# One encoder layer on one core: output weights split during the column pairs, and a new order of copies, sums and operands in the projection

## The reference, cut to what matters

```python
h = rms_norm(x, p['g_mix'][l])
proj = h @ p['w_in'][l]
hq, hf_fwd, hf_bwd, hi, hg, dq, dk, dv = jnp.split(proj, points, axis=-1)
q_hg = silu(hq);  f = lb + (1 - lb) * sigmoid(fx);  gates = log(f), 1 - f     # fx: hf_fwd, hf_bwd
...
x = x + mix @ p['w_out'][l]
```

## Time and profile before

| What | Value |
|---|---|
| Median of 3 runs | 2064.74 us (2061.48 to 2066.44) |
| The profiled execution | 2061.51 us; its span 2059.7 us |
| TensorE busy | 1958.7 us, 95% |
| VectorE, ScalarE, POOL busy | 72%, 60%, 15% |
| Token steps; column pairs | 0 to 210 us; 210 to 470 us |

### The profile page before, as it was taken

How to read it: one execution, slowest core, us unless ns; L and a number is a source line. 1 busy time by engine, 2 the same in 40 slices (tenths; PEclk the granted TensorE clock), 3 DMA queues, 4 the chain that set the end, 5 groups by cost and what they waited for, 6 DMA issues and landing times. The chain is left out here.

```text
span 2059.7 us, 31859 instructions
## 1 busy us (share of the span) xinstructions
PE 1958.7 (95%) x11162; PEld 1620.1 (79%) x11162; DVE 1491.5 (72%) x2050; ACT 1237.7 (60%) x1974; POOL 307.7 (15%) x394
## 2 busy tenths in 40 slices
PE   7988999999999899999999999999999999999983
PEld 6876887887888667778887888887888888888871
DVE  5347665648999588877311455578999999999976
ACT  5442466526788498744322433327888888888863
POOL 0220012110000021111000000001223332222210
PEclk9999999999999999999999999999999999999997
DMA  6492333446655451334334322448999999999988
GB/s 211 165 308 93 103 123 133 144 161 181 185 177 174 155 191 38 103 134 149 104 123 161 122 101 91 154 150 315 384 384 379 382 376 379 381 385 393 378 310 325
DMA packets 178389, 448.27 MB, mean 218 GB/s; under 512 B 21152, under 2 KB 100384, under 8 KB 151648
## 3 DMA queue, kind: packets, MB, share of 16 engines
q1 hardware_dynamic: 146032, 347.48, 47.3%
q0 software_dynamic: 32240, 99.25, 13.2%
HBM read 366.46 MB, written 94.90 MB: 224 GB/s over the span
## 5 line engine op out<-in xcount | busy, mean ns | idle before, releaser
L113 PE MATMUL cross_ot_ps<-w_w_high,cross_o_high 128*128 128x512 f32 x544 | 219.9, 404 | 2.1 <-DVE w_w_low L2932 1.6
L115 PE MATMUL cross_ot_ps<-w_w_high,cross_o_low 128*128 128x512 f32 x544 | 213.3, 392 | 0.0
L2932 DVE TENSOR_TENSOR cross_low_up<-cross_raw_up,w_w_high 128x2048 fp32r<-128x2048 f32 x68 | 152.8, 2289 | 12.4 <-ACT w_w_high L2716 12.2
L2932 DVE TENSOR_TENSOR cross_low_down<-cross_raw_down,w_w_low 128x2048 fp32r<-128x2048 f32 x68 | 152.7, 2287 | 1.7 <-ACT w_w_low L2716 1.7
L2932 DVE TENSOR_TENSOR w_w_low<-cross_raw_gate,w_w_high 128x2048 fp32r<-128x2048 f32 x68 | 152.3, 2279 | 0.0
L2716 ACT ACTIVATE w_w_high<-cross_raw_up 128x2048 fp32r<-128x2048 f32 x68 | 126.2, 1906 | 0.3 <-issue 0.3
L2716 ACT ACTIVATE w_w_low<-cross_raw_down 128x2048 fp32r<-128x2048 f32 x68 | 126.2, 1906 | 0.0
L2716 ACT ACTIVATE w_w_high<-cross_raw_gate 128x2048 fp32r<-128x2048 f32 x68 | 126.0, 1901 | 0.0
L113 PEld LDWEIGHTS cross_ot_ps<-w_w_high,cross_o_high 128*128 128x128 f32 x544 | 102.9, 189 | 28.7 <-DVE w_w_low L2932 7.1
L115 PEld LDWEIGHTS cross_ot_ps<-w_w_high,cross_o_low 128*128 128x128 f32 x544 | 102.7, 189 | 22.2
L113 PE MATMUL cross_out_ps<-w_w_low,cross_ht 128*128 128x512 f32 x272 | 109.5, 402 | 5.6 <-DVE cross_low_down L2932 5.6
(11 more groups left out here) (515 smaller groups left out, 5573.1 us busy)
## 6 DMA issues: line engine op xcount, KB each, us to landing
cross_raw_gate<-in_w_gate_dram SPq DMA_DIRECT2D x68, 1024.0 KB, 6.7
cross_raw_down<-in_w_down_dram SPq DMA_DIRECT2D x68, 1024.0 KB, 7.6
cross_raw_up<-in_w_up_dram SPq DMA_DIRECT2D x68, 1024.0 KB, 8.8
front_pair_raw<-in_w_in_dram SPq DMA_DIRECT2D x9, 1024.0 KB, 5.8
cross_y_kept<-y_rows SPq DMA_DIRECT2D x16, 512.0 KB, 9.2
front_raw<-in_w_in_dram SPq DMA_DIRECT2D x10, 512.0 KB, 4.9
k_t<-front_staged POOLq DMA_DIRECT2D x20, 256.0 KB, 2.4
lf_t<-front_staged_lf POOLq DMA_DIRECT2D x20, 256.0 KB, 3.1
```

The costliest lines, as they stand in the source:

```text
L113: pe.matmul(out, lhs[0], rhs[0], start=first, stop=False)
L115: return pe.matmul(out, lhs[1], rhs[0], start=False, stop=last)
L2932: dve.tensor_tensor(w_low[s][:, cols], raw[s][:, cols], w_high[s][:, cols].bitcast(F32), ALU.subtract).then_inc(w_low_done[s], 1)
```

## The change

Output weights: the tiles of `w_out` get no turn in the g steps. They are split in pairs 6 to 9, at three places of a pair's order: place 0 ahead of slot 1, place 1 after slot 3 (ScalarE) or after the first chunk's finish (VectorE), place 2 after slot 6. Pair 6 takes tiles 0 and 1 at places 1 and 2, pair 7 tiles 2 and 3 at the same, pair 8 tiles 4, 5 and 6, pair 9 tile 7 at place 1. They have one buffer for raw and low (the same memory) and one for high, and SP loads a tile when the one before it has been stored. SP's loads stand between its others: tiles 0 and 1 ahead of the weights of pair 9, tiles 2 to 4 after the first key weights, 5 and 6 after the first operands of the scan, 7 after the second, ahead of the memory's loads. POOL's stores stand after chunks 0, 1 and 4. The key weights are loaded to two places, the second one once all slots are ready.

Token steps: a bank's copy comes ahead of the rounding of a token sum, and slots ahead of S3. Column pairs: ScalarE makes the sigmoid of chunk 1 ahead of slot 4; VectorE makes u3, c22 and u4 after slot 2 and ahead of slot 3, and finishes chunk 0 after that.

The diff, cut to its core (semaphore lists left out):

```diff
@@ -201,9 +201,10 @@
     first_mem = tiles
-    out_rounds = {tiles: (0, 1), tiles + 1: (2, 3), tiles + 2: (4,), tiles + 3: (5, 6), tiles + 4: (7,)}
     pairs = [(kind, j) for kind in BY_COLUMN for j in range(HEADS // 2)]
     last_pair = len(pairs) - 1
+    out_rounds = {p: rounds for p, rounds in enumerate(((None, 0, 1), (None, 2, 3), (4, 5, 6), (None, 7, None)), len(pairs) - 4)}
+    out_round = lambda p, place: out_rounds.get(p, (None,) * 3)[place]
     sig_pairs = sum(kind in SIGMOIDS for kind, _ in pairs)
@@ -234,10 +235,10 @@
         xn = (m.over("xn_even", at + 86016, [P, D]), m.over("xn_odd", at + 94208, [P, D]))
-        out_raw = m.over("out_raw", at + 90112, [P, 2, 2, group_size])
-        out_low = m.over("out_low", at + 90112, [P, 2, 2, group_size], F32R)
+        out_raw = m.over("out_raw", at + 114688, [P, 2, group_size])
+        out_low = m.over("out_low", at + 114688, [P, 2, group_size], F32R)
+        out_high = m.over("out_high", at + 118784, [P, 2, group_size], F32R)
         mem_tile = m.over("mem_tile", at + 98304, [P, 2, KC, P], F32R)
-        out_high = m.over("out_high", at + 106496, [P, 2, 2, group_size], F32R)
         ones = m.over("ones", early, [DK, P])
@@ -250,7 +251,7 @@
         staged_lf = m.over("staged_lf", at + 120832, [P, 3, HALF])
-        next_raw = m.over("next_raw", at + 114688, [P, 2, KC, P])
+        next_raw = [m.over(f"next_raw{i}", at + (122880, 163840)[i], [P, KC, P]) for i in range(2)]
         chunk_of = staged[:].rearrange("p u t -> p (u t)").rearrange("p (c t) -> p c t", c=CHUNKS_OF_PAIR)
@@ -364,13 +365,14 @@
                 def load_out(r):
-                    if r < 2:
-                        sp.wait_ge(xn_done, NT)
-                        sp.wait_ge(turned, NT)
+                    if r == 0:
+                        sp.wait_ge(part_done, CHUNKS_OF_PAIR * sig_pairs)
+                        for u in range(3):
+                            sp.wait_ge(lf_stored[u], 16 * ((gate_chunks - u + 2) // 3))
                     else:
-                        sp.wait_ge(out_stored[r % 2], 32 * (r // 2))
-                    sp.dma_start(out_raw[:, r % 2], w_out[r * P:(r + 1) * P, :].rearrange("p (a n) -> p a n", a=2)
-                                 ).then_inc(out_in[r % 2], 16)
+                        sp.wait_ge(out_stored, 32 * r)
+                    sp.dma_start(out_raw[:], w_out[r * P:(r + 1) * P, :].rearrange("p (a n) -> p a n", a=2)
+                                 ).then_inc(out_in, 16)

@@ -385,13 +387,9 @@

-                def load_next():
-                    sp.wait_ge(part_done, CHUNKS_OF_PAIR * sig_pairs)
-                    for u in range(3):
-                        sp.wait_ge(lf_stored[u], 16 * ((gate_chunks - u + 2) // 3))
-                    for p in range(2):
-                        sp.dma_start(next_raw[:, p], w_next[:, p * P:(p + 1) * P].rearrange("(k p) n -> p k n", p=P)
-                                     ).then_inc(next_in, 16)
+                def load_next(p):
+                    sp.dma_start(next_raw[p][:], w_next[:, p * P:(p + 1) * P].rearrange("(k p) n -> p k n", p=P)
+                                 ).then_inc(next_in, 16)

@@ -424,24 +422,30 @@
                 load_mem(0)
-                load_out(0)
-                load_out(1)
                 load_chunk(2 * chunks + 1)
...
                         load_chunk(2 * chunks + 1 + j)
-                    load_out(2 * j)
-                    load_out(2 * j + 1)
                 for p in range(len(pairs)):
                     load_pair(p)
-                load_next()
+                    if p == last_pair - 1:
+                        load_out(0)
+                        load_out(1)
+                load_next(0)
+                load_out(2)
+                load_out(3)
+                load_out(4)
                 for c in range(CHUNKS_OF_PAIR):
...
                 load_first_x(0)
+                load_out(5)
+                load_out(6)
                 sp.wait_ge(slot_ready, 8 * len(pairs))
+                load_next(1)
                 load_first_x(1)
+                load_out(7)
                 for u in range(2):
@@ -516,10 +520,8 @@
                 def round_out(r):
-                    act.wait_ge(out_in[r % 2], 16 * (r // 2 + 1))
-                    if r >= 2:
-                        act.wait_ge(out_stored[r % 2], 32 * (r // 2))
-                    act.activation(out_high[:, r % 2], out_raw[:, r % 2], ACT.Copy).then_inc(out_high_done, 1)
+                    act.wait_ge(out_in, 16 * (r + 1))
+                    act.activation(out_high[:], out_raw[:], ACT.Copy).then_inc(out_high_done, 1)

@@ -609,42 +611,46 @@
                         find_mem_rstd(n - first_mem)
+                    if kind in SILUS:
+                        wide_sigmoid(n)
+                    else:
+                        copy_out(n)
                     if n == first_step[2]:
...
                     if n == first_step[2] + 1:
-                        round_s(S3)
                         for i in range(8):
                             round_slot(0, i)
+                        round_s(S3)
                     if n == first_step[2] + 3:
...
                         round_s(S4)
-                    if kind in SILUS:
-                        wide_sigmoid(n)
-                    else:
-                        copy_out(n)
-                    for r in out_rounds.get(n, ()):
-                        round_out(r)

...
                     round_next(p, 0)
+                    if out_round(p, 0) is not None:
+                        round_out(out_round(p, 0))
                     round_next(p, 1)
...
                     round_next(p, 3)
+                    if out_round(p, 1) is not None:
+                        round_out(out_round(p, 1))
+                    sigmoid(p, 1)
                     round_next(p, 4)
...
                         for i, (_, high_of, _) in enumerate(next_split):
-                            act.activation(high_of[:], next_raw[:, i], ACT.Copy).then_inc(next_high_done, 1)
+                            act.activation(high_of[:], next_raw[i][:], ACT.Copy).then_inc(next_high_done, 1)
                     copy_sample(p)
-                    sigmoid(p, 1)
                     round_next(p, 6)
+                    if out_round(p, 2) is not None:
+                        round_out(out_round(p, 2))
                     sigmoid(p, 2)
@@ -700,7 +706,7 @@
                     dve.wait_ge(out_high_done, r + 1)
-                    dve.tensor_tensor(out_low[:, r % 2], out_raw[:, r % 2], out_high[:, r % 2].bitcast(F32),
+                    dve.tensor_tensor(out_low[:], out_raw[:], out_high[:].bitcast(F32),
                                       ALU.subtract).then_inc(out_low_done, 1)
@@ -860,12 +866,8 @@
                     wide_silu(n)
-                    for r in out_rounds.get(n, ()):
-                        subtract_out(r)

                 dve.wait_ge(turned, NT + mem_tiles)
-                for u in range(2):
-                    dve.wait_ge(out_stored[u], 32 * (KC // 2))
                 combine(S1, bottom[:, 0], bottom[:, 1], ALU.add)
@@ -883,25 +885,32 @@
                     finish(p - 1, 4)
+                    if out_round(p, 0) is not None:
+                        subtract_out(out_round(p, 0))
                     prepare(p + 1, 1)
...
                     make_u2(p)
-                    finish(p, 0)
-                    prepare(p + 1, 2, 3)
+                    prepare(p + 1, 2)
                     make_u3(p)
...
                     clamp(p, 1)
+                    prepare(p + 1, 3)
+                    finish(p, 0)
+                    if out_round(p, 1) is not None:
+                        subtract_out(out_round(p, 1))
                     prepare(p + 1, 4, 5)
...
                             dve.wait_ge(next_high_done, i + 1)
-                            dve.tensor_tensor(low_of[:], next_raw[:, i], high_of[:].bitcast(F32), ALU.subtract)
+                            dve.tensor_tensor(low_of[:], next_raw[i][:], high_of[:].bitcast(F32), ALU.subtract)
                     make_c12(p)
...
                     prepare(p + 1, 6)
+                    if out_round(p, 2) is not None:
+                        subtract_out(out_round(p, 2))
                     make_c21(p)
@@ -1071,7 +1080,7 @@
                         pool.dma_start(out_split[part, r * P:(r + 1) * P, :].rearrange("p (a n) -> p a n", a=2),
-                                       split[:, r % 2].bitcast(F32)).then_inc(out_stored[r % 2], 16)
+                                       split[:].bitcast(F32)).then_inc(out_stored, 16)

@@ -1088,8 +1097,6 @@
                                    staged[:, u, 0:2 * HW].rearrange("p (r c) -> p r c", c=HW)).then_inc(stored[u], 16)
-                    for r in out_rounds.get(n, ()):
-                        store_out(r)

@@ -1106,7 +1113,11 @@
                         store_chunk(p, c)
+                        if c in (0, 1, 4) and out_round(p, (0, 1, 4).index(c)) is not None:
```

(11 more changed lines are left out.)

## The result

The changed kernel takes 2074.54 us (median of 5 runs, 2072.56 to 2078.96) against 2064.74 us: a ratio of 1.0051, 95% interval [1.0036, 1.0066]. The forecast was 2059.5, 2046 to 2071. The execution profiled is the slowest of the five, 2078.96 us with a span of 2077.2; of its 17.5 us over the span of before, 10.9 are there when the next stage begins, near the 9.8 us between the medians. Its granted clock is 0.93 in the stretch from 900 to 1000 us behind that point, 0.97 in those.

A forecast was written before the change was run, and what follows sets the result against it. TensorE, busy 95% of 2059.7 us, was taken as the bound. Gains of 19.8 and 5.6 us less a loss of 20.2 left 5.2: from 2061.5 to 2056.3, given as 2059.5 for the median of runs; range 2046 to 2071.

The forecast's parts named there:

- Token steps: Ten steps before pair 0: TensorE's waits and lower clock there go, gaining 19.8 us, bounds 16 to 20.
- Gate pairs: Pairs 3 to 5: third sums 27.8 us apart instead of 29.34, shorter waits, gain 5.6 us, bounds 3 and 8.
- Rival 3: Gate-pair edit fails: third sum still waits for ScalarE's slot 2, sums still 29 apart; 2063 us; chance 0.08.
- The link: Output-weight chain in pairs 6 to 9, one tile's rounding to the next through one buffer: 10.7 us, bounds 10.4 and 14.5.
- Rivals 1: Output-weight chain is hidden, tile 4 ready 6.6 us sooner, end wait shrinks too; 2046 to 2053 us; chance 0.14.
- rival 2: Output-weight loads by SP in the pairs take 5.5 us, not 3.6; 8 us slower, 2073; chance 0.18.
- The store of tile 1: Its landing beside pair and key weights, taken as 6 us, putting tile 2 at 413.
- Pairs 8 and 9: TensorE waits 6.6 us for pair 8's third sum, loses 1.6 to the clock, then 2.3 before pair 9's product.
- the tail: After the last matmul: memory loads behind tile 7 land at about 486, next stage 9.7 us later.

## Why the prediction was wrong

- **Token steps: right.** 19.8 us forecast, 20.3 found, no wait left. The kernel with the output weights alone shows that 19.4 of them come from the move and not from the copy order.
- **Gate pairs: right.** Third sums 27.8 us apart, found 27.77 (313.08 to 340.85); waits of 1.6 and 2.8 us, found 1.67 and 2.68; gain 5.6, found 5.3 (pair 0 to pair 6 takes 155.4 us for 160.7). Rival 3 falls.
- **The link: right where nothing crosses.** 10.7 us, found 10.8 to 11.0; loads landed in 3.1 to 4.0 us, median 3.6. The Trainium skill's formula ("DMA: Bandwidth & Descriptors", "Anatomy of one DMA") gives 3.2 for this size, but for transfers that GpSimd issues: the first stores of a tile took 3.0 to 3.3 us where little else moved, so there the trace agrees. SP issues the loads, and for them the row was nearer. Rivals 1 and 2 both fall: loads of 5.5 us were not what made it slow, and that rival 2's 2073 lies near the measured time is chance.
- **The store of tile 1: too small.** I gave it 6 us for the crossing with pair and key weights; its parts took 8.2 and 9.9. Tile 2 came at 397.2 for 393.2 (the forecast's 413 less 19.8), and all that follows hangs on it. So what I had called covered in pair 7 was not: c21, behind tile 3's subtraction on VectorE, ended at 411.1 and not 407.1, and TensorE stood 2.46 us.
- **Pairs 8 and 9: right in kind, near in size.** 6.6 us by a partial sum of VectorE's, found 7.29; 2.3 us, found 1.68. The lower clock was counted once, 1.6 us; pairs 6 to 9 lost 15.6 us with waits of 11.4, so 4.2. With pair 7's wait, pairs 6 to 9 cost 5.1 us more than the 10.5 forecast.
- **The step that failed: the tail.** "The next stage begins 12.3 us after the last matmul: 9.7 us more." (12.3 less the 2.8 of before is 9.5.) It began 23.7 us after it, 20.9 more. I had seen that GpSimd would wait for store 7 and priced that at nothing, since the memory lands at about the same time. But the drain behind that wait takes 7.2 us and stood hidden in the kernel before; a wait at the end of an engine's list has to be priced with what the engine still does after it. The other 4 us are that the last store landed 14.9 us after the last matmul. The stores of tile 6 took 6.7 and 7.6 us beside key weights and scan operands, and those of tile 7 took 8.8 and 10.7 beside the memory loads; I had used 3.8. The two errors need each other. By the forecast's own times store 7 lands at about 481.6 (loaded 471, 3.6 for the load, 7.0 to the landing), and a drain of 7.2 us behind that ends 2.8 us after the memory's 486 (an estimate): late stores made the whole drain count.
- **Sum.** Forecast: 25.4 gained, 20.2 lost. Found: 25.6 gained, 36.5 lost. The 16.3 us between the losses are 11.2 of the tail and 5.1 of the pairs, and the sign turned. The range was too narrow for this: its slow end came from slower loads alone and had no case in which the drain counts.

Only argued, not tested: that the 1.0 us by which GpSimd's drain of 7.2 us exceeds the 6.2 of before comes from its stores having landed just ahead of it. Open: why the granted clock of the profiled execution of the changed kernel is lower in one later stretch; it is the slowest of its five.

## What to carry over

Moving work into a stage where the engines are idle is free only if its transfers are, too: eight tiles through one buffer made a chain of 11 us and more a tile, and a second buffer took away every wait of TensorE that it caused. At the end of a stage, ask which engine ends last and what its queue does after its last wait; here 6 to 7 us of GpSimd's drain were free in one kernel and fully paid in the other, and handing the last store to another queue gave 5 us. When two changes are bundled, price them apart: the orders alone were worth 12.8 us, and the move hid that. They don't add up either, since copy order and move took away the same waits. As it was written the move cost 24.5 us on top of the orders; with two buffers and the last store on SyncE it was worth 4.9 (2045.18 for 2050.05).

## What was not expected of the hardware

GpSimd's drain at the end of a block took 6.2 us where its transfers had long landed (6196 ns in all six kernels, begun between 436.6 and 469.5), 7.2 us just behind its last landing, 8.1 and 8.9 with the stores of tile 6 issued 3 and 2 us before, and 13.8 us with two stores just issued, ending 3.4 us after they landed. SyncE's took 7 ns (118 once).
